# A pool-and-conv mixer inside a two-model kernel: pooled means moved from VectorE to GpSimd, with the last eight input tiles, the small pool products and the residual's norm in a new order

## Chip, cores and metric

The kernel runs on one core of a Trainium2 chip. The metric is the device time of one execution in microseconds. A profiled execution gives a span from its first to its last instruction; the execution's own time is a little longer, as the table below says.

## What is computed

The reference is a chain of two blocks over 256 positions of 1024 channels in f32: a first block (convolution, latent attention, a gated FFN and a final norm), then a second with a pool-and-conv mixer, an FFN, windowed attention and a mixture of eight experts. Only the mixer and what stands around it are touched:

```python
h = rmsnorm(x, ev_norm_mix); x = x + pool_conv_mixer(h, ...)
h = rmsnorm(x, ev_norm_ffn); x = x + swiglu(h, ...)

def pool_conv_mixer(h, w_in, pool_w, pool_scale, conv_w, w_out):
    proj = h @ w_in                                   # 1024 -> 2048
    u, gate_post, gate_pre, v = split(proj, 4)        # 512 channels each
    y_a = multiscale_pool(u, pool_w, pool_scale)
    y_b = gate_post * causal_depthwise_conv(gate_pre * v, conv_w)   # 3 taps
    return concatenate([y_a, y_b]) @ w_out            # 1024 -> 1024

def multiscale_pool(u, pool_w, pool_scale):           # windows 2, 4, 8, 16
    # per group of 128 channels with its window w:
    #   pooled = (sum of the last w positions) / min(t + 1, w) - u
    #   mixed  = pooled @ pool_w[group]               # 128 x 128
    return mixed * pool_scale
```

The `x` that enters the mixer is the first block's result under its final norm `norm_f_g`.

## The kernel before

**Layout.** Channels lie on the 128 partitions and the 256 positions along the free axis. A linear layer is a row of jobs; a job is one output tile of 128 channels x 256 positions in one PSUM bank (`jb(n)` is bank n mod 4). Each f32 product is made of three matmuls (`three`, L711 to L713): high by high, high by low and low by high, where high is an fp32r copy and low is what is left. A job of eight row tiles is 24 matmuls of 128x256.

**Weights.** They come in granules of 128x2048 f32 (1 MB) on SP's queue, six buffers deep. ScalarE writes the high half `whi` (L1144) and VectorE the low half `wlo` (L1516), three buffers deep. In the mixer a granule serves two jobs. `split_to(g)` makes all halves up to two granules beyond g. ScalarE's copy waits until the granule three back has been used up; SP's load into a buffer waits until VectorE's half of its last content is done. `split_past(n)` goes one further where job n is the last of its granule.

**Order of the mixer.** The order on every engine is written out by hand; engines meet at semaphores. Jobs `mix`+0 to 7 are pairs of gate_pre and v tiles; `mix`+8 to 15 are pairs of a gate_post and a u tile (called tiles 9 to 16 below). A job may start once the one four before it, which had its bank, has been drained (`drained`, `wait_drained`).
- *VectorE, first half.* After two statistics on bank 7 it makes `rsq` (L1795 to L1797). For each of four conv groups it drains two jobs (`pre`, L1605, and `z`, L1825) and makes the three taps in `zc` (L1827, L1829) and a scale (L1833). Between them stand `mid_norm` (a second variance, L1808, and the reciprocal `rlat`, L1813) and two calls of `normalise_two`, each of two L1803, which put the final norm of the first block into the residual `xres`.
- *VectorE, second half.* Four groups i = 0 to 3 (L1835 to L1862). Each makes its weight split, `yb` from PSUM (L1839), waits for ScalarE's high copy and writes the low half, drains u into `pu` (L1605), sums windows by doubling (L1854, i + 1 times, between `pa` and `pb`), multiplies by `recip` (L1856), subtracts (L1859, `pooled`), and waits for ScalarE's copy of the pool product before it writes its low half (L1861). `pu`, `pa`, `pb`, `pooled` and `yb` are one buffer each. Groups 2 and 3 also hold a `normalise_two`.
- *ScalarE.* For each group the weight copy, the high half of `yb` (L1322), and the scaled high half of the pool product from bank 6 (L1324).
- *TensorE.* Tile 9, tile 10, tile 11, pool product 0 (L914, `pool_mix`), tile 12, tile 13, pool product 1, and so on; product 3 stands after tile 16. Then the eight jobs of `mix_out`, whose operands are `mh` and `ml`.
- *Residual.* For each output tile VectorE adds PSUM to `xres` (L1743) and writes the low half of the next operand (L1558); ScalarE makes its high half and squares (L1162, L1163), and GpSimd sums the squares (L576). The next layer, `up2`, begins with two jobs together that need all eight operand tiles only at their end (`job_pair`).
- *GpSimd.* Sums of squares, here for the norms, DMAs of tables, and nothing between 410 and 487 us. It has no part in the mixer.

## Time and profile before

| | |
|---|---|
| median of 3 runs | 1789.27 us (1789.26 to 1790.92) |
| profiled execution, its own time | 1788.94 us |
| its span | 1787.1 us, mean granted TensorE clock 0.981 |
| TensorE matmul busy | 1704.0 us, 95%, 10076 instructions |
| VectorE busy | 1424.9 us, 80%, 1409 instructions |
| ScalarE busy | 1145.4 us, 64%, 1143 instructions |
| GpSimd busy | 148.4 us, 8%, 137 instructions |
| DMA | 513.47 MB, mean 287 GB/s |

PE is TensorE's matmuls, DVE VectorE, ACT ScalarE, POOL GpSimd, SP SyncE; L711 is line 711 of the kernel. Times are microseconds from the span's start. A matmul's shown duration (0.28 us at full clock) is longer than the spacing at which matmuls follow each other. The granted clock is a share of full speed; its two levels are 1.2 and 2.4 GHz. VectorE's instructions overlap by some 0.08 us where none waits for the other.

### The profile page before, as it was taken

Reading aid. Unit: us, or ns where it says so; the run is one execution under the profiler, and the core shown is the slowest. Engines: PE = TensorE matmul, PEld = TensorE weight load, DVE = VectorE, ACT = ScalarE, POOL = GpSimd, SP = SyncE. Lnnn points to the kernel's source line nnn. Section 1 sums busy time; section 2 is a strip of 40 time slices with the busy share of each in tenths; the row PEclk is TensorE's granted clock in tenths of the full one; section 3 lists DMA queues with packets and bytes.
Section 4 is the critical chain, followed back from the end, with each engine's and each line's share of the span. In section 5 each row is a group of like instructions: output and inputs, shape, how many; then the busy total and the mean of one; then the engine's idle time right before and its main releaser. Section 6 shows DMA issues by size and latency. Waiting matters only on the chain.

```text
span 1787.1 us, 26233 instructions
## 1 busy us (share of the span) xinstructions
PE 1704.0 (95%) x10076; PEld 1509.3 (84%) x10076; DVE 1424.9 (80%) x1409; ACT 1145.4 (64%) x1143; POOL 148.4 (8%) x137
## 2 busy tenths in 40 slices
PE   7899999998799998979999999999999999999994
PEld 6888999998799998877888888888888888888883
DVE  7896788857666656758888888888888888888886
ACT  5325577753344444647787787787877877878774
POOL 5000255410010001010000000000000000000000
PEclk9999999999899999999999999999999999999997
DMA  8334496594345557139999999999999999999994
GB/s 310 105 140 172 159 396 265 197 248 173 106 178 189 181 197 218 48 141 367 382 369 389 368 373 389 368 379 379 360 403 367 361 397 374 368 380 366 395 384 152
DMA packets 75037, 513.47 MB, mean 287 GB/s; under 512 B 7984, under 2 KB 8368, under 8 KB 16720
## 3 DMA queue, kind: packets, MB, share of 16 engines
q1 hardware_dynamic: 68688, 487.65, 71.4%
q0 software_dynamic: 6272, 24.76, 4.9%
q8 instruction: 52, 0.85, 0.2%
q14 instruction: 25, 0.20, 0.0%
HBM read 488.26 MB, written 24.12 MB: 287 GB/s over the span
## 4 chain that ended last, share of the span: by engine, by line
PE 87%; DVE 6%; ACT 3%; issue 1%; POOL 1%; DMA 1%; DVEq 0%; POOLq 0%; SPq 0%; ACTq 0%
PE psum L711 27%; PE psum L713 26%; PE psum L712 26%; PE psum L762 3%; DVE wlo L1516 2%; PE psum L1078 1%; ACT whi L1144 1%; DVE acc L1599 0%; PE psum L1049 0%; PE psum L953 0%; PE psum L840 0%; PE psum L861 0%; PE psum L801 0%; POOL ang L613 0%; DMA yrow<-expert_outs,idx 0%
## 5 line engine op out<-in xcount | busy, mean ns | idle before, releaser
L1516 DVE TENSOR_TENSOR wlo<-wraw,whi 128x2048 fp32r<-128x2048 f32 (+1 forms) x446 | 1014.5, 2278 | 210.6 <-ACT whi L1454 117.0
L1454 ACT ACTIVATE whi<-wraw 128x2048 fp32r<-128x2048 f32 x336 | 643.4, 1917 | 213.1 <-PE psum L713 213.1
L711 PE MATMUL psum<-whi,xgh 128*128 128x512 f32 x896 | 357.7, 399 | 1.8 <-DVE xgl L1516 1.8
L713 PE MATMUL psum<-whi,xgl 128*128 128x512 f32 x896 | 351.4, 392 | 0.0
L712 PE MATMUL psum<-wlo,xgh 128*128 128x512 f32 x896 | 349.1, 390 | 0.0
L711 PE MATMUL psum<-ah,whi 128*128 128x256 f32 x1064 | 307.3, 289 | 4.3 <-DVE u L1605 1.7
L712 PE MATMUL psum<-al,whi 128*128 128x256 f32 x1064 | 303.9, 286 | 0.0
L713 PE MATMUL psum<-ah,wlo 128*128 128x256 f32 x1064 | 303.6, 285 | 0.0
L1144 ACT ACTIVATE whi<-wraw 128x2048 fp32r<-128x2048 f32 x105 | 200.3, 1910 | 121.5 <-PE psum L713 121.5
L711 PEld LDWEIGHTS psum<-ah,whi 128*128 128x128 f32 x1064 | 207.3, 195 | 5.9 <-DVE wlo L1516 1.9
L712 PEld LDWEIGHTS psum<-al,whi 128*128 128x128 f32 x1064 | 207.1, 195 | 0.4
L713 PEld LDWEIGHTS psum<-ah,wlo 128*128 128x128 f32 x1064 | 207.0, 195 | 0.0
L713 PEld LDWEIGHTS psum<-whi,xgl 128*128 128x128 f32 x896 | 168.2, 188 | 39.3
L711 PEld LDWEIGHTS psum<-whi,xgh 128*128 128x128 f32 x896 | 168.5, 188 | 36.5 <-issue 2.0
L712 PEld LDWEIGHTS psum<-wlo,xgh 128*128 128x128 f32 x896 | 168.5, 188 | 35.0
L711 PE MATMUL psum<-whi,ath 128*128 128x512 f32 x448 | 177.8, 397 | 0.0
L713 PE MATMUL psum<-whi,atl 128*128 128x512 f32 x448 | 175.6, 392 | 0.0
L712 PE MATMUL psum<-wlo,ath 128*128 128x512 f32 x448 | 174.4, 389 | 0.0
L713 PEld LDWEIGHTS psum<-whi,atl 128*128 128x128 f32 x448 | 84.1, 188 | 19.6
L712 PEld LDWEIGHTS psum<-wlo,ath 128*128 128x128 f32 x448 | 84.2, 188 | 18.0
L711 PEld LDWEIGHTS psum<-whi,ath 128*128 128x128 f32 x448 | 84.2, 188 | 16.8
L711 PE MATMUL psum<-fh,whi 128*128 128x256 f32 x352 | 97.5, 277 | 0.0
(329 smaller groups left out, 2095.6 us busy)
## 6 DMA issues: line engine op xcount, KB each, us to landing
wraw<-weights SPq DMA_DIRECT2D x454, 1024.0 KB, 6.9
expert_rows<-zeros POOLq DMA_DIRECT2D x1, 8704.0 KB, 43.6
expert_outs<-ysb SPq DMA_DIRECT2D x9, 512.0 KB, 9.1
expert_outs<-zeros POOLq DMA_DIRECT2D x1, 4096.0 KB, 59.8
xgt<-expert_rows SPq DMA_DIRECT2D x8, 512.0 KB, 8.7
bias_rows<-ttab POOLq DMA_DIRECT2D x1, 3072.0 KB, 37.4
btab<-bias_rows POOLq DMA_DIRECT2D x2, 768.0 KB, 10.4
xres<-x SPq DMA_DIRECT2D x1, 1024.0 KB, 5.2
```

Of the source, the lines that this page charges most:

```text
L711: nc.tensor.matmul(out, lh, rh, start=start, stop=False)
L712: nc.tensor.matmul(out, lh, rl, start=False, stop=False)
L713: return nc.tensor.matmul(out, ll, rh, start=False, stop=stop)
L762: mm = nc.tensor.matmul(jb(n), wraw[:, g % NW, off:off + P], x[:, k, :], start=(k == 0), stop=(k == PLAN.jobs[n][-1][2]))
L1078: mm = nc.tensor.transpose(bank[6][:, i * P:(i + 1) * P], act_[:, i * P:(i + 1) * P], ident)
L1144: sc.activation(whi[:, i % NS, :], wraw[:, g % NW, :], ACT.Copy).then_inc(hi_done, 1)
L1454: sc.activation(whi[:, (GS + j) % NS, :], wraw[:, g % NW, :], ACT.Copy).then_inc(hi_done, 1)
L1516: return ve.tensor_tensor(dst, value, hi.bitcast(f32), SUB)
```

## The change

Group q of the second half is now channel group i = 3 - q, so the longest window comes first, and the u tile comes before the gate_post tile (`make_plan`). GpSimd zeroes the edges of `z`, `pu`, `pa` and `pb` and makes the window sums, the multiply and the subtract; each step waits for the one before. `pu` and `pooled` have a buffer for each group and `yb` two, at places that hold the first FFN's operands before. VectorE multiplies u by `rstd` into `pu`, and writes the low half of `yb` one group later and that of the pool product two groups later. TensorE makes products 0 and 1 between the tiles of groups 2 and 3, into banks 4 to 7 instead of bank 6, and products 2 and 3 between parts of the first two output tiles, whose rows are taken in the order 7, 6, 5, 3, 2, 4, 1, 0. ScalarE's copies follow that order. The reciprocal `rlat` stands after the four conv groups, and the four `normalise_two` stand in the residual of `mix_out`. VectorE no longer waits for `table_rep` and `late`; GpSimd waits for `late`.

```diff
@@ -151 +151 @@
         p.tile("ev_w_in_2", KD, spread(1536 + i * P, P))
-    for i in range(4):
+    for i in range(3, -1, -1):
+        p.tile("ev_w_in_2", KD, spread(i * P, P))
         p.tile("ev_w_in_2", KD, spread(512 + i * P, P))
-        p.tile("ev_w_in_2", KD, spread(i * P, P))
     linear("mix_out", "ev_w_out_2", KD, KD)
@@ -373 +373 @@
         PP = 16 + T
-        pa = place("pa", [P, PP], f32, 10 * KB + 256)
-        pb_ = place("pb", [P, PP], f32, 11 * KB + 512)
-        pu = place("pu", [P, PP], f32, 12 * KB + 768)
-        pooled = place("pooled", [P, T], f32, 14 * KB)
-        yb = place("yb", [P, T], f32, 15 * KB)
+        pu = place("pu", [P, 4, PP], f32, 40 * KB)
+        pa = place("pa", [P, PP], f32, 44 * KB + 512)
+        pb_ = place("pb", [P, PP], f32, 45 * KB + 768)
+        pooled = place("pooled", [P, 4, T], f32, 47 * KB)
+        yb = place("yb", [P, 2, T], f32, 51 * KB)
 
@@ -664 +666 @@
                     add(rlat[:], rlat[:], sq2[:, c % 2, :], summed2)
+            wait_job(pool, AT["down1"] + KD - 1)
+            pool.memset(z[:, :, 0:2], 0.0)
+            pool.memset(pu[:, :, 0:16], 0.0)
+            pool.memset(pa[:, 0:16], 0.0)
+            pool.memset(pb_[:, 0:16], 0.0).then_inc(edges_set, 1)
+            pool.wait_ge(late, 32)
+            pool.wait_ge(edges_set, 1)
+            windows = [0]
+
+            def window(ins):
+
+                ins.then_inc(window_step, 1)
+                windows[0] += 1
+                pool.wait_ge(window_step, windows[0])
+
+            for q in range(4):
+                i = 3 - q
+                pool.wait_ge(u_copied, q + 1)
+                src, dst = pu[:, i, :], pa
+                for step in range(i + 1):
+                    sh = 1 << step
+                    window(nc.gpsimd.tensor_tensor(dst[:, 16:PP], src[:, 16:PP], src[:, 16 - sh:PP - sh], ADD))
+                    src, dst = dst, (pb_ if dst is pa else pa)
+                window(nc.gpsimd.tensor_tensor(dst[:, 16:PP], src[:, 16:PP], recip[:, i, :], MUL))
+                nc.gpsimd.tensor_tensor(pooled[:, i, :], dst[:, 16:PP], pu[:, i, 16:PP], SUB).then_inc(pooled_done, 1)
+                pool.wait_ge(pooled_done, q + 1)
             for name in ("h4", "od"):
@@ -907 +935 @@
 
-            def pool_mix(i):
-                pe.wait_ge(pooled_done, i + 1)
-                if i:
-                    pe.wait_ge(m_lo, KD + 2 * i)
-                nc.tensor.matmul(bank[6][:, 0:T], poolw[:, i, :], pooled[:, :], start=True, stop=True).then_inc(pool_mm, 1)
-
-            for i in range(4):
-                job(AT["mix"] + 8 + 2 * i, ah, al)
-                if i:
-                    pool_mix(i - 1)
-                job(AT["mix"] + 9 + 2 * i, ah, al)
+            def pool_mix(q):
+
+                i = 3 - q
+                pe.wait_ge(pooled_done, q + 1)
+                if q == 3:
+                    pe.wait_ge(stat_read, stat[0])
+                nc.tensor.matmul(bank[4 + q][:, 0:T], poolw[:, i, :], pooled[:, i, :],
+                                 start=True, stop=True).then_inc(pool_mm, 1)
+
+            for q in range(4):
+                job(AT["mix"] + 8 + 2 * q, ah, al)
+                if q >= 2:
+                    pool_mix(q - 2)
+                job(AT["mix"] + 9 + 2 * q, ah, al)
+
+            mixed = (7, 6, 5, 3, 2, 4, 1, 0)
+
+            def mixed_ready(k):
+
+                return (p_lo, 4 - k) if k < 4 else (y_lo, 8 - k)
+
+            def mix_part(n, ks):
+
+                if ks[0] == mixed[0]:
+                    wait_drained(pe, n - 4)
+                for k in ks:
+                    g, off, _ = PLAN.jobs[n][k]
+                    once(lo_done, TURN[g] + 1)
+                    once(*mixed_ready(k))
+                    s = TURN[g] % NS
+                    mm = three(jb(n), whi[:, s, off:off + P], wlo[:, s, off:off + P], mh[:, k, :], ml[:, k, :],
+                               k == mixed[0], k == mixed[-1])
+                if ks[-1] == mixed[-1]:
+                    mm.then_inc(jobs_done, 1)
+                    at_piece[0] += 1
+
+            mix_part(AT["mix_out"], mixed[:3])
+            pool_mix(2)
+            mix_part(AT["mix_out"] + 1, mixed[:3])
+            mix_part(AT["mix_out"], mixed[3:6])
             pool_mix(3)
-
-            for i in range(KD):
-                job(AT["mix_out"] + i, mh, ml, lambda k: (m_lo, KD + (2 * k + 2 if k < 4 else 2 * (k - 4) + 1)))
+            mix_part(AT["mix_out"] + 1, mixed[3:6])
+            mix_part(AT["mix_out"], mixed[6:])
+            mix_part(AT["mix_out"] + 1, mixed[6:])
+            for i in range(2, KD):
+                job(AT["mix_out"] + i, mh, ml)
             job_pair(AT["up2"], ah, al, lambda k: (h_lo, 3 * KD + k + 1))
@@ -1315 +1374 @@
                 split_to(last_granule(AT["mix"] + 2 * i))
-            for i in range(4):
-                n = AT["mix"] + 8 + 2 * i
-                split_to(last_granule(n))
-                act.wait_ge(yb_done, i + 1)
-                sc.activation(mh[:, 4 + i, :], yb[:], ACT.Copy).then_inc(m_hi, 1)
-                act.wait_ge(pool_mm, i + 1)
-                sc.activation(mh[:, i, :], bank[6][:, 0:T], ACT.Copy, scale=pcol("ev_pool_scale_2", i)).then_inc(m_hi, 1)
+            def pool_hi(q):
+
+                i = 3 - q
+                act.wait_ge(pool_mm, q + 1)
+                sc.activation(mh[:, i, :], bank[4 + q][:, 0:T], ACT.Copy,
+                              scale=pcol("ev_pool_scale_2", i)).then_inc(p_hi, 1)
+
+            for q in range(4):
+                split_to(last_granule(AT["mix"] + 8 + 2 * q))
+                if q >= 2:
+                    pool_hi(q - 2)
+                act.wait_ge(yb_done, q + 1)
+                sc.activation(mh[:, 7 - q, :], yb[:, q % 2, :], ACT.Copy).then_inc(y_hi, 1)
+            pool_hi(2)
+            pool_hi(3)
             take("mix_out", lambda c: pcol("ev_norm_ffn_2", c))
@@ -1733 +1800 @@
 
-            def residual(phase, gain=None, bias=None):
+            def residual(phase, gain=None, bias=None, ahead=None):
 
...
                     split_to(last_granule(n))
+                    if ahead is not None:
+                        v.wait_ge(norm_done, i + 1)
                     wait_job(v, n)
@@ -1746 +1815 @@
                         operand_low(i - 1, gain)
+                    if ahead is not None and i % 2 == 0 and i + 2 < KD:
+                        ahead(i // 2 + 1)
                     if i < KD - 1:
@@ -1785 +1856 @@
 
-            v.wait_ge(table_rep, 16)
-            ve.memset(z[:], 0.0)
-            ve.memset(pb_[:], 0.0)
-            link(ve.memset(pu[:, 0:16], 0.0))
             split_to(last_granule(AT["mix"]))
@@ -1808 +1875 @@
                 v.sem_inc(stat_read, 1)
-                link(ve.memset(pa[:], 0.0))
-                v.wait_ge(rstd_sqrt, 2)
-                link(ve.reciprocal(rlat[:], var[:]))
 
...
                     mid_norm()
-                elif i > 1:
-                    normalise_two(i - 2)
                 n = AT["mix"] + 2 * i
@@ -1824 +1886 @@
                 wait_drained(v, n + 1)
+                if i == 0:
+                    v.wait_ge(edges_set, 1)
                 link(ve.tensor_scalar(zc[:, i, :], z[:, i, 0:T], pcol("ev_conv_w_2", i), None, MUL))
@@ -1831 +1895 @@
                 link(ve.tensor_tensor(zc[:, i, :], zc[:, i, :], rstd[:], MUL))
-            v.wait_ge(late, 32)
-            for i in range(4):
-                n = AT["mix"] + 8 + 2 * i
+            v.wait_ge(rstd_sqrt, 2)
+            link(ve.reciprocal(rlat[:], var[:]))
+
+            def gated_low(q):
+
+                v.wait_ge(y_hi, q + 1)
+                lo(ml[:, 7 - q, :], yb[:, q % 2, :], mh[:, 7 - q, :]).then_inc(y_lo, 1)
+
+            def pool_low(q):
+
+                i = 3 - q
+                v.wait_ge(p_hi, q + 1)
+                ve.scalar_tensor_tensor(ml[:, i, :], bank[4 + q][:, 0:T],
+                                        pcol("ev_pool_scale_2", i), mh[:, i, :].bitcast(f32), MUL, SUB).then_inc(p_lo, 1)
+
+            for q in range(4):
+                n = AT["mix"] + 8 + 2 * q
+                i = 3 - q
+                wait_job(v, n)
+                ve.tensor_tensor(pu[:, i, 16:PP], jb(n), rstd[:], MUL).then_inc(u_copied, 1)
+                v.wait_ge(u_copied, q + 1)
+                v.sem_inc(drained[n % 4], 1)
+                if q:
+                    gated_low(q - 1)
                 split_to(last_granule(n))
-                wait_job(v, n)
-                link(ve.tensor_tensor(yb[:], jb(n), zc[:, i, :], MUL))
-                v.sem_inc(drained[n % 4], 1)
-                v.sem_inc(yb_done, 1)
-                v.wait_ge(m_hi, KD + 2 * i + 1)
-                lo(ml[:, 4 + i, :], yb[:], mh[:, 4 + i, :]).then_inc(m_lo, 1)
-
-                if i:
-                    v.wait_ge(pooled_done, i)
-                if i >= 2:
-                    normalise_two(i)
-                drain(n + 1, pu[:, 16:PP])
-                wait_drained(v, n + 1)
-                src, dst = pu, pa
-                for step in range(i + 1):
-                    sh = 1 << step
-                    link(ve.tensor_tensor(dst[:, 16:PP], src[:, 16:PP], src[:, 16 - sh:PP - sh], ADD))
-                    src, dst = dst, (pb_ if dst is pa else pa)
-                link(ve.tensor_tensor(src[:, 16:PP], src[:, 16:PP], recip[:, i, :], MUL))
-                if i:
-                    v.wait_ge(pool_mm, i)
-                ve.tensor_tensor(pooled[:], src[:, 16:PP], pu[:, 16:PP], SUB).then_inc(pooled_done, 1)
-                v.wait_ge(m_hi, KD + 2 * i + 2)
-                ve.scalar_tensor_tensor(ml[:, i, :], bank[6][:, 0:T], pcol("ev_pool_scale_2", i),
-                                        mh[:, i, :].bitcast(f32), MUL, SUB).then_inc(m_lo, 1)
-            v.wait_ge(norm_done, KD)
-            residual("mix_out", lambda c: pcol("ev_norm_ffn_2", c))
+                if q >= 2:
+                    pool_low(q - 2)
+                wait_job(v, n + 1)
+                ve.tensor_tensor(yb[:, q % 2, :], jb(n + 1), zc[:, i, :], MUL).then_inc(yb_done, 1)
+                v.wait_ge(yb_done, q + 1)
+                v.sem_inc(drained[(n + 1) % 4], 1)
+            gated_low(3)
+            pool_low(2)
+            pool_low(3)
+            normalise_two(0)
+            residual("mix_out", lambda c: pcol("ev_norm_ffn_2", c), ahead=normalise_two)
             inverse_std(D, rstd)
...
```

## Rows read from the trace of the kernel before

**Rows 1.** The page, chain that ended last: share of the span by engine.

```profile
PE 87%; DVE 6%; ACT 3%; issue 1%; POOL 1%; DMA 1%; DVEq 0%; POOLq 0%; SPq 0%; ACTq 0%
```

**Rows 2.** Busy time by stretch: PE, PEld, DVE, ACT, POOL, clock, DMA share, GB/s.

```profile
407.00:440.00 33.00, 32.78 (x269) 32.36 (x267) 28.98 (x45) 12.58 (x11) 1.43 (x2) 1.00 0.43 150
440.00:484.00 44.00, 29.48 (x177) 28.07 (x177) 26.82 (x44) 11.58 (x14) 0.00 (x0) 0.77 0.31 106
...
540.00:640.00 100.00, 100.00 (x841) 100.00 (x840) 62.98 (x85) 43.69 (x53) 0.00 (x0) 1.00 0.52 180
```

**Rows 3.** Who waited for whom, 405 to 505 us: total, times, longest.

```profile
ACT mh L1324 <- PE psum L914: 17.8, 4, 5.7
ACT mh L1322 <- DVEq L1841: 17.5, 4, 8.9
...
PE psum L914 <- DVE pooled L1859: 14.5, 4, 5.1
```

**Rows 4.** TensorE in order of time: start, us, line, operation, idle before.

```profile
413.03 0.59 PE L904 MATMUL psum<-rlat,ones 128*128 128x256 f32 x2
...
439.94 0.28 PE L713 MATMUL psum<-ah,wlo 128*128 128x256 f32 x1
444.94 1.22 PE L914 MATMUL psum<-pooled,poolw 128*128 128x256 f32 x2 [4.71 <-DVE pooled L1859]
...
449.37 0.41 PE L712 MATMUL psum<-al,whi 128*128 128x256 f32 x1
...
475.83 1.22 PE L914 MATMUL psum<-pooled,poolw 128*128 128x256 f32 x2 [5.13 <-DVE pooled L1859]
...
483.65 0.28 PE L713 MATMUL psum<-mh,wlo 128*128 128x256 f32 x1
```

**Rows 5.** VectorE in order of time, 410 to 446 us.

```profile
413.02 0.92 DVE L1789 MEMSET z<- 128x1032 f32 x1 [0.16 <-issue]
...
414.29 0.42 DVE L1795 TENSOR_SCALAR var<-psum 128x256 f32<-128x256 f32 x1
...
422.66 2.29 DVE L1516 TENSOR_TENSOR wlo<-wraw,whi 128x2048 fp32r<-128x2048 f32 x1
...
439.48 2.29 DVE L1516 TENSOR_TENSOR wlo<-wraw,whi 128x2048 fp32r<-128x2048 f32 x1
```

**Rows 6.** Groups of instructions, 410 to 484 us: busy us, mean ns.

```profile
L1803 DVE SCALAR_TENSOR_TENSOR xres<-xres,par,rlat 128x256 f32<-128x256 f32 x8 | 3.5, 480 | 0.1
...
L1854 DVE TENSOR_TENSOR pa<-pu 128x256 f32<-128x256 f32 x4 | 1.7, 427 | 0.1
```

**Rows 7.** GpSimd, and VectorE where they meet, in order of time.

```profile
20.79 0.74 POOL L614 TENSOR_TENSOR ang<-ang 128x256 f32<-128x256 f32 x1
21.61 0.85 POOL L613 TENSOR_SCALAR ang<-ang 128x256 f32<-128x256 f32 x1
22.55 0.74 POOL L614 TENSOR_TENSOR ang<-ang 128x256 f32<-128x256 f32 x1
22.75 2.68 DVE L1516 TENSOR_TENSOR wlo<-wraw,whi 128x2048 fp32r<-128x2048 f32 x1
...
27.59 2.77 POOL L617 TENSOR_SCALAR ang<-ang 128x256 f32<-128x256 f32 x1
...
409.51 0.73 POOL L576 TENSOR_TENSOR rlat<-rlat,sq 128x256 f32<-128x256 f32 x1
...
486.33 2.29 DVE L1516 TENSOR_TENSOR wlo<-wraw,whi 128x2048 fp32r<-128x2048 f32 x1 [1.19 <-ACT whi L1144]
487.08 2.14 POOL L576 TENSOR_TENSOR ssum<-sq 128x256 f32<-128x256 f32 x1 [76.84 <-ACT sq L1163]
```

**Rows 8.** TensorE behind two earlier idle stretches, in order of time.

```profile
45.04 0.39 PE L711 MATMUL psum<-ah,whi 128*128 128x256 f32 x1 [1.68 <-DVE u L1605]
...
193.95 0.58 PE L711 MATMUL psum<-mh,whi 128*128 128x256 f32 x1 [2.58 <-DVE gates L1725]
```

**Rows 9.** ScalarE's weight copy in the loop, in order of time.

```profile
431.45 1.92 ACT L1144 ACTIVATE whi<-wraw 128x2048 fp32r<-128x2048 f32 x1 [4.32 <-PE psum L713]
```

More of the change, by code:

```diff
@@ L476, in program @@
         pooled_done, pool_mm, yb_done = sem("pooled_done"), sem("pool_mm"), sem("yb_done")
+        y_hi, y_lo, p_hi, p_lo = sem("y_hi"), sem("y_lo"), sem("p_hi"), sem("p_lo")
+        edges_set, window_step = sem("edges_set"), sem("window_step")
         table_mm, table_out, table_rep, bias_ready = sem("table_mm"), sem("table_out"), sem("table_rep"), sem("bias_ready")
```

## The prediction, made before the change was run

> **What bounds the kernel now.** The page first: TensorE holds 87% of the chain that ended last [rows 1]; only stretches where it is idle or slow can give time. The table by stretches then shows where one is [rows 2]: from 540 to 640 us it is busy all of 100 us with 841 matmuls (0.12 us each, 2.88 us for a tile of 24) at granted clock 1.00; from 440 to 484 us, where the change works, it is busy 29.5 of 44 us at a mean clock of 0.77, with VectorE at 26.8 and the DMA engines at 0.31, so neither is full: a stretch of waits. The waits name them [rows 3]: TensorE's pool products (L914) wait 14.5 us, four times, for `pooled` of VectorE; ScalarE's copies wait 17.8 us for those products and 17.5 us for `yb`. The order of time shows the loop [rows 4]: the last matmul before the first product starts at 439.94, the first and the fourth product at 444.94 and 475.83 after 4.71 and 5.13 us of idleness, and output tiles 1 and 2 end at 483.9. At 449.37 a matmul still takes 0.41 us, against 0.28 before the idle stretch: the lower level, 1.2 GHz. VectorE starts a weight split at 439.48 [rows 5], and in this loop needs 9 to 11 us a group (two tiles) where TensorE needs 5.8.
>
> So from the end of mixer tile 11 (440.0) to the end of output tile 2 (483.9) pass 43.9 us. At full clock and without waits it would be 5 mixer tiles and 2 output tiles, 7 x 2.88 = 20.2 us, and four products of 0.66, 2.6 us: 22.8. **21.1 us are to be had**, 14.5 of idleness and 6.6 of lower clock.
>
> **Part by part.**
>
> *Before the eight tiles.* Three memsets go from VectorE to GpSimd: 0.92 us [rows 5] and two small ones. What is late next is TensorE's statistic, which ends at 413.6 [rows 4] against VectorE's start on it at 414.29 [rows 5]: gain 0.6. The reciprocal of 1.75 us moves behind the fourth conv group; the split that followed it at 422.66 then waits for ScalarE, which makes its high half only after its second square root, so all of this gives 0.65. Two pairs of L1803 (0.48 us each) go too, 1.8 us [rows 6], but the reciprocal comes back ahead of the first u tile: VectorE takes that tile at about 439.0. TensorE, which waited there three times for a drain, ends tile 11 at 439.3: **0.7 us gained**. GpSimd's four memsets (bound below by nothing; above by the 0.92 us of the whole `z`, 3.7 in all) begin behind its sum that ends at 410.2 [rows 7] and are wanted at 416.9: they cost nothing under 6.7 us together; beyond that VectorE's first conv step would wait for them.
>
> *Pooled means.* Ten window adds, four multiplies and four subtracts leave VectorE, 18 x 0.43 = 7.7 us [rows 6]. On GpSimd an add of this size takes 0.74 us alone, and with the wait behind it the next starts after 0.82 (20.79 and 21.61) [rows 7]. The multiply and the subtract of two tensors get the price of the add: nearest row, same operands; bounds 0.74 and the 2.77 of a step that met a split. Groups run with windows 16, 8, 4, 2: 6, 5, 4 and 3 steps, 14.8 us unhindered. They meet VectorE's splits: the sum at 487.08 took 2.14 us, ending 0.6 after the split begun at 486.33, and a split begun at 22.75, 0.2 us after a GpSimd add, took 2.68 instead of 2.29 [rows 7]. One waits until the other has finished, in either direction; operations with a PSUM input (0.41) keep their time.
>
> The Trainium skill (SBUF — State Buffer, SBUF: two separate sides) calls this port pair an exclusive lock on which the loser fully blocks; the rows agree.
>
> *First chain.* u tile 0 is copied at 439.4; VectorE starts the split of the mixer's seventh granule (m6) at the same moment. First add ends at 441.7 + 0.6 = 442.3; adds 2 to 4 end at 443.1, 444.0, 444.8; the multiply falls under the next split (VectorE 444.4 to 446.9, held up 0.25) and ends at 447.5; the subtract at 448.3. TensorE meanwhile does tiles 12 and 13 of the mixer and is out of work at 445.0, since pool product 0 stands ahead of tile 14. **Idle for 3.3 us.** Afterwards the clock: earlier, an idle stretch of 2.58 us was followed by a first matmul of 0.58 us, one of 1.68 us by one of 0.39 [rows 8]. 3.3 lies beyond the longer, so I take the lower level for about 4.6 us, as behind 444.94 [rows 4]: some 19 matmuls at 0.213 instead of 0.12 and a product at 1.2: **2.2 us**. If the clock stays up, that is 0; both ends go into the range.
>
> *Following chains.* TensorE goes on at 448.3: product 0 (1.2), tile 14 until 454.2, tile 15 until 457.0, product 1, tile 16 until 460.5, three of eight rows of output tile 1 (9 matmuls, 1.1) until 461.6, product 2, three rows each of output tiles 2 and 1 until 464.4, product 3, and the rest until 467.6. GpSimd's second chain runs from 448.3 with one split in between, five steps, to 454.3: hidden. The third has its u since 447.7, four steps, 457.4: hidden by 4 us. The fourth gets its u from tile 15 at 457.6, meets a split until 460.8 and is done at 462.2: hidden by 2.
>
> *VectorE and ScalarE in the loop.* VectorE has per group a split (2.29) and four short operations (0.42 to 0.48, as in [rows 6]): 4.0 us, under 5.8 even with 0.6 for each of two meetings. What it now queues behind p_hi and y_hi, ScalarE delivers a group later; ScalarE has 1.92 [rows 9] and two short copies a group. Its waits for the pool product sit behind the split, and product 0 (448.9) is over before that split is (449.5). The SP queue: each load is released by a split's end, so loads come earlier with the rest; share 0.31 becomes about 0.5, which is what the later stretch has at full pace [rows 2]. No DMA is added or moved, and GpSimd's next ones belong to the attention, far behind. VectorE's wait for the bias table goes; that write had landed.
>
> *Residual's norm.* Four pairs of L1803, formerly two among the conv groups and two in the loop, now stand in the residual: one pair (0.88) before tile 1, the others behind tiles 0, 2, 4. The residual then has per two tiles a split 2.29, two adds and two lows at 0.42 to 0.48 (1.8), a pair 0.96, with one more meeting with GpSimd's sums (0.6): 5.65 against 5.76 of TensorE. Tight: VectorE enters it at 466, behind the last pooled low, and the last lows come about 0.3 us after up2's first pair of jobs wants them (before, they were there in time). **0.3 us lost.**
>
> **Sum.** 43.9 us become 22.8 + 3.3 + 2.2 = 28.3, gain 15.6; plus 0.7, less 0.3: **16.0 us**. Against the profiled execution's 1788.94 us that is 1773.0; the median of the runs, 1789.27, lies 0.3 above it, so I give **1773.2**. All behind runs on TensorE at full pace [rows 2] and moves forward as a block.
>
> **Rivals.**
> *Gapless.* GpSimd slips its first add in ahead of m6, no later step meets a split, or the idleness stays short enough for the clock. Chain: 6 x 0.82 = 4.9 us, done at 444.3 to 445.5. Gain 21.1 + 0.7 - 0.3, less at most 2 for single meetings: -19.5 to -21.5, 1768 to 1770. Against it: a split stands right behind the u copy in the queue, and ScalarE's half for it is ready.
> *The port eats it.* Each step on GpSimd excludes VectorE's two-SBUF-input work, so the 14.8 us come back on VectorE in place of the 7.7 removed: 7.1 us more, gain 9, **1780**. For: both directions show in [rows 7]. Against: VectorE has some 1.8 us a group to spare, and its PSUM operations pass. The Trainium skill (Perfetto Trace Analysis, Optimizing Scalar/DVE Operations) says that moving work between these two might not help because of the shared port; by that the time would be this one or worse.
> *Slower.* The chain of GpSimd, in order and linked, becomes the bound: all steps near the price of a collision, 2.5 us (between 2.14 and 2.77). 439.4 + 18 x 2.58 = 485.8, then product, ScalarE, VectorE and the rows of the output tiles left, some 5.2: 491 against 483.9, **+7, 1796**. It decides from about 2 us a step. Against: VectorE's splits fill 2.3 of 5.8 us, and most steps must run between them.
> *Does nothing.* Something else, such as ScalarE's order, holds the loop at its old pace: 1789. Nothing in [rows 3] speaks for it once `pooled` is gone.
>
> **Chances.** Forecast 0.58 (1770.5 to 1776.5), gapless 0.13, port 0.20, slower 0.05, nothing 0.04. The range takes forecast, gapless and most of port: 1768 to 1780.5. A measurement tells about 0.2% (3.6 us) from no change: faster 0.92, same 0.04, slower 0.04.
>
> **What the profile after should show.** Right: L914 idle before it about 3.3 us in one place, none over 1 elsewhere; 440 to 484 at clock about 0.95; GpSimd's 18 steps at 0.74, five or six of them 2 us or more; output tile 2's end near 467.6; up2 in step 16 us earlier. Wrong: product 1 to 3 waiting for POOL (port or slower), splits well over 2.7 us, or TensorE waiting for `al` at up2 by more than 1 us.

## The result and the profile after

The changed kernel takes **1773.3 us** (median of 4 runs, 1771.28 to 1774.46) against 1789.26 us (4 runs, 1789.16 to 1790.92), a ratio of 0.9906 with a 95% interval of [0.9894, 0.9918]: 16.0 us less, where 1773.2 was forecast. Its profiled execution took 1774.46 us (span 1772.3, clock 0.981), 14.5 less than that of before. TensorE holds 89% of the chain that ended last, against 87% in [rows 1].

The table by stretches, columns as in [rows 2]:

```profile
407.00:440.00 33.00, 33.00 (x275) 32.89 (x274) 25.87 (x38) 12.59 (x11) 1.66 (x6) 1.00 0.45 160
440.00:484.00 44.00, 41.08 (x333) 40.66 (x332) 32.19 (x43) 20.64 (x27) 27.34 (x23) 0.96 0.46 168
540.00:640.00 100.00, 100.00 (x850) 100.00 (x849) 60.97 (x77) 44.10 (x51) 1.48 (x2) 1.00 0.53 184
```

From 440 to 484 us TensorE is busy 41.1 of 44 us, not 29.5, with 333 matmuls in place of 177, and its mean clock is 0.96, not 0.77. The waits from 405 to 490 us show what is left:

```profile
ACT mh L1389 <- DVE yb L1926: 19.5, 4, 9.3
DVE wlo L1583 <- ACT whi L1203: 13.2, 10, 2.7
...
PE psum L944 <- POOL pooled L693: 2.9, 1, 2.9
...
ACT mh L1381 <- PE psum L944: 2.7, 2, 2.1
...
PE psum L739 <- DVE al L1625: 1.0, 1, 1.0
```

Against [rows 3]: TensorE waits for `pooled` once and 2.9 us, not four times and 14.5; ScalarE waits 2.7 us for the small products, not 17.8. ScalarE's long wait for `yb` is still there (19.5) and costs nothing by these rows: VectorE makes the low half from this `mh` one group later and waits 0.5 us for it once, and TensorE never waits for it. The one new wait of TensorE is for `al`, 1.0 us. GpSimd in order of time has all 18 steps of the pooled means; the first group, the other long steps and the last:

```profile
440.26 2.74 POOL L690 TENSOR_TENSOR pa<-pu 128x256 f32<-128x256 f32 x1 [29.12 <-DVE pu L1917]
443.07 0.61 POOL L690 TENSOR_TENSOR pb<-pa 128x256 f32<-128x256 f32 x1
443.76 0.71 POOL L690 TENSOR_TENSOR pa<-pb 128x256 f32<-128x256 f32 x1
444.55 0.73 POOL L690 TENSOR_TENSOR pb<-pa 128x256 f32<-128x256 f32 x1
445.37 2.65 POOL L692 TENSOR_TENSOR pa<-pb,recip 128x256 f32<-128x256 f32 x1
448.10 0.73 POOL L693 TENSOR_TENSOR pooled<-pa,pu 128x256 f32<-128x256 f32 x1
...
450.35 2.54 POOL L690 TENSOR_TENSOR pa<-pb 128x256 f32<-128x256 f32 x1
...
458.40 2.67 POOL L692 TENSOR_TENSOR pb<-pa,recip 128x256 f32<-128x256 f32 x1
461.14 0.74 POOL L693 TENSOR_TENSOR pooled<-pb,pu 128x256 f32<-128x256 f32 x1
```

Four steps take 2.54 to 2.74 us, each begun 0.03 to 0.6 us behind the start of a weight split of VectorE; the other fourteen take 0.61 to 0.74. TensorE behind the first product:

```profile
448.88 0.70 PE L944 MATMUL psum<-pooled,poolw 128*128 128x256 f32 x2 [2.92 <-POOL pooled L693]
...
449.53 0.29 PE L740 MATMUL psum<-al,whi 128*128 128x256 f32 x1
449.65 0.38 PE L741 MATMUL psum<-ah,wlo 128*128 128x256 f32 x1
449.83 0.42 PE L739 MATMUL psum<-ah,whi 128*128 128x256 f32 x1
...
456.65 0.59 PE L944 MATMUL psum<-pooled,poolw 128*128 128x256 f32 x2
...
463.55 0.60 PE L944 MATMUL psum<-pooled,poolw 128*128 128x256 f32 x2
```

Beside [rows 4]: there the first, third and fourth product took 1.22 us, at the lower level, and the second 0.70. Here the one behind the idle stretch takes 0.70, the others 0.59 to 0.60, and the lower level (0.42 us a matmul) begins only at 449.7 and ends at 453.0.

**The stage measured by itself.** To read the experiments I use one length in each profile: from the start of the mixer's second statistics product on TensorE (L904 before, L932 after) to that of up2 (L801, L829). It holds all that the change touches but the memsets of the edges on GpSimd (410.9 to 411.2 us). What stands behind it is read in two lengths that no edit touches: from there to VectorE's first work on the attention's keys (`kk`), 190.3 to 190.4 us in every profile, and from `kk` to its first work on the experts' result rows (`yrow`), called "attention to experts" below.

| | before | after |
| --- | --- | --- |
| start | 413.03 | 413.70 |
| to the end of tile 11 | 27.03 | 26.34 |
| from there to the end of output tile 2 | 44.07 | 26.35 |
| from there to up2's statistic | 22.71 | 23.72 |
| **stage** | **93.81** | **76.41** |
| attention to experts | 1075.1 | 1076.7 |

The stage gained 17.4 us. It began 0.7 later, attention to experts took 1.6 more, the rest of the span 0.2 and what lies around the span 0.4: 14.5 are left in the profiled execution. In the thirteen profiles of this document the stage begins anywhere between 411.9 and 416.2 us, so a difference of 0.7 there says nothing of the change.

### The profile page after: what moved, and what is told of

It reads as the page before. It is cut to its first block, busy times and chain, and to the rows that moved or that the text cites. A ratio compares the mean times of both kernels' runs of the same rounds, so it can differ in the third digit from the quotient of the medians.

```text
span 1772.3 us, 26239 instructions
## 1 busy us (share of the span) xinstructions
PE 1701.3 (96%) x10076; PEld 1507.5 (85%) x10076; DVE 1416.5 (80%) x1387; ACT 1145.0 (65%) x1143; POOL 168.7 (10%) x159
## 4 chain that ended last, share of the span: by engine, by line
PE 89%; DVE 5%; ACT 2%; POOL 2%; issue 1%; DMA 1%; DVEq 0%; POOLq 0%; SPq 0%; ACTq 0%
PE psum L739 27%; PE psum L741 27%; PE psum L740 26%; PE psum L790 3%; PE psum L1137 1%; DVE wlo L1583 1%; ACT whi L1203 1%; DVE acc L1666 0%; PE psum L1108 0%; PE psum L1012 0%; PE psum L868 0%; PE psum L889 0%; PE psum L829 0%; POOL ang L615 0%; PE psum L1019 0%
## 5 line engine op out<-in xcount | busy, mean ns | idle before, releaser
L739 PEld LDWEIGHTS psum<-whi,ath 128*128 128x128 f32 x448 | 84.3, 188 | 16.3
```

Source lines behind the costliest of these rows:

```text
L739: nc.tensor.matmul(out, lh, rh, start=start, stop=False)
```

## The experiments

Of each kernel the median of 4 runs is given (of 10 for the eighth), its ratio to the kernel before on the same chip with the 95% interval, and the stage of its profile. The kernel before, beside them, had medians of 1788.92, 1790.02 and 1790.48 us.

**1. The means back on VectorE, all else kept**

```diff
# GpSimd: the loop over q with its window steps and waits is gone; on VectorE, behind each u copy
+                if q == 0:
+                    v.wait_ge(late, 32)
+                src, dst = pu[:, i, :], pa
+                for step in range(i + 1):
+                    link(ve.tensor_tensor(dst[:, 16:PP], src[:, 16:PP], src[:, 16 - sh:PP - sh], ADD))
...
+                link(ve.tensor_tensor(dst[:, 16:PP], src[:, 16:PP], recip[:, i, :], MUL))
+                ve.tensor_tensor(pooled[:, i, :], dst[:, 16:PP], pu[:, i, 16:PP], SUB).then_inc(pooled_done, 1)
```

> The changed kernel with its order, buffers and late products, but the 18 window steps back on VectorE, each group's behind its u copy. Theory A (the order pays: products two groups late, own buffers): product 0 is ready some 6 us earlier (6 steps of 0.46 us, no port), TensorE instead waits about 1.7 us for the low half of the seventh granule, which now stands behind 2.8 us of steps; VectorE has 6.8, 6.3, 5.8 and 5.4 us a group against 5.76. About the changed kernel's time, 1773 (1771 to 1776). Theory B (the gain is the work taken off VectorE): VectorE becomes the bound again, most of the gain goes, 1780 to 1789.

1773.86 us (1771.92 to 1775.47), ratio 0.9914 [0.9897, 0.993]; stage 76.70, 0.3 more than after. The waits and the stretch:

```profile
PE psum L718 <- DVE wlo L1562: 2.2, 1, 2.2
...
PE psum L718 <- DVE al L1604: 1.0, 1, 1.0
...
PE psum L718 <- DVE ml L1562: 0.6, 1, 0.6
```

```profile
440.00:484.00 44.00, 40.27 (x322) 39.34 (x320) 38.37 (x60) 20.87 (x29) 8.45 (x5) 0.96 0.48 168
```

No wait for `pooled` at all: VectorE has the first group ready in time, and in exchange is late with one split (2.2 us) and with one `ml` (0.6). It is busy 38.4 us of 44 rather than 32.2, and that still suffices. **The engine is not what pays.** What pays lies in the order, the buffers and the lateness of the small work. The lateness is priced by number 2 and the norm pairs by 7 and 8; the order of the windows and the buffers of their own were not tried alone.

**2. Products and low halves one group late**

```diff
-                if q >= 2:
-                    pool_mix(q - 2)
+                if q >= 1:
+                    pool_mix(q - 1)
...
+            pool_mix(3)
```

with the same for `pool_hi` on ScalarE and `pool_low` on VectorE.

> Means on GpSimd as in the changed kernel, but each product one group earlier, where the kernel before has them (product 3 behind tile 16), and ScalarE's and VectorE's halves of it likewise. Theory A: product 0 stands behind tile 11 and waits for the GpSimd chain until 448.8: some 9 us idle, and two later products wait about a microsecond or two: 7 us slower than the changed kernel, 1780 (1777 to 1784). Theory B (work off VectorE pays, the place of the products does not): 1773 to 1775.

1778.9 us (1778.48 to 1782.27), ratio 0.9947 [0.993, 0.9963]; stage 82.89, **6.5 us longer** than after.

```profile
PE psum L944 <- POOL pooled L693: 10.5, 2, 8.7
```

GpSimd's chain is as long as before, but TensorE meets it one tile pair earlier and waits 8.7 us at once. A first chain of 8.6 us (440.26 to 448.8 in the changed kernel) can be hidden only behind more than one group of 5.8 us. With the means on VectorE, where number 1 has the first group ready 2.7 us after its first window step, one group might be enough; that was not tried, so the 6.5 us hold for the chain on GpSimd.

**3. The first product behind tile 14**

```diff
-                if q >= 2:
-                    pool_mix(q - 2)
+                if q == 3:
+                    pool_mix(1)
                 job(AT["mix"] + 9 + 2 * q, ah, al)
+                if q == 2:
+                    pool_mix(0)
```

> Changed kernel with product 0 behind tile 14 instead of ahead of it. Theory C (TensorE's idle stretch of 2.9 us and the lower clock behind it, 1.4 us, are simply lost time): 4 us faster, 1769. Theory D (the GpSimd chain of all four groups, without a gap from the first u copy to the last subtract, some 22 us, sets when the stretch ends): the idle time moves to product 1 (about 2.5 us, for its pooled at 454.4) and the time stays, 1773.

1773.19 us (1771.55 to 1773.99), ratio 0.9908 [0.9892, 0.9925]; stage 75.88, 0.5 less. Product by product on TensorE:

```profile
448.41 0.70 PE L944 MATMUL psum<-pooled,poolw 128*128 128x256 f32 x2
...
454.08 1.22 PE L944 MATMUL psum<-pooled,poolw 128*128 128x256 f32 x2 [2.11 <-POOL pooled L693]
```

The first product no longer waits, the second does (2.1 us). The position of the product is not the limit; the second chain runs straight behind the first, and both are late by when the first began.

**4. Subtract only.** This kernel leaves the window additions and the multiply by `recip` out of the pooled means; one GpSimd step a group is left.

```diff
-                for step in range(i + 1):
+                for step in range(0):
...
-                nc.gpsimd.tensor_tensor(pooled[:, i, :], dst[:, 16:PP], pu[:, i, 16:PP], SUB).then_inc(pooled_done, 1)
+                nc.gpsimd.tensor_tensor(pooled[:, i, :], recip[:, i, :], pu[:, i, 16:PP], SUB).then_inc(pooled_done, 1)
```

> Leaves out the window adds and the multiply: GpSimd only subtracts u from the reciprocal counts, 4 steps instead of 18, so the pooled means are other values. This prices the whole chain and its meetings at the port. Theory D: product 0 no longer waits, clock stays up, splits are not held up: 4 us faster than the changed kernel, 1769 to 1770. Rival (the port eats it): splits and low halves were held up much more than the trace shows, 7 us or more faster, 1766 or less. If nothing of it counted: 1773.

1769.54 us (1769.16 to 1772.44), ratio 0.9894 [0.9877, 0.991]; stage 72.66. So the fourteen steps left out, with their meetings and the clock, cost **3.75 us** of the stage and no more. The stretch is at full clock throughout, and `al` is waited for 0.3 us:

```profile
440.00:484.00 44.00, 42.97 (x351) 42.14 (x351) 34.37 (x47) 23.21 (x32) 16.04 (x11) 1.00 0.51 183
```

**5. The reciprocal back where VectorE idles.** The change moved it (1.75 us) from the middle of the conv groups to ahead of the first u copy. VectorE after, in order of time:

```profile
419.92 0.42 DVE L1875 TENSOR_SCALAR var<-psum 128x256 f32<-128x256 f32 x1
422.63 2.29 DVE L1583 TENSOR_TENSOR wlo<-wraw,whi 128x2048 fp32r<-128x2048 f32 x1 [2.29 <-ACT whi L1203]
...
437.87 1.75 DVE L1899 RECIPROCAL rlat<-var 128x256 f32<-128x256 f32 x1
439.66 0.42 DVE L1917 TENSOR_TENSOR pu<-psum,rstd 128x256 f32<-128x256 f32 x1
```

It idles for 2.29 us at 420.3, and holds up the u copy by 1.75 at 437.87.

```diff
                 v.sem_inc(stat_read, 1)
+                v.wait_ge(rstd_sqrt, 2)
+                link(ve.reciprocal(rlat[:], var[:]))
...
-            v.wait_ge(rstd_sqrt, 2)
-            link(ve.reciprocal(rlat[:], var[:]))
```

> Changed kernel with the reciprocal of 1.75 us back in the middle norm, where VectorE has 2.3 us idle for ScalarE's weight copy. Theory D (what sets the stretch's end is when the GpSimd chain begins): the first u copy comes 1.75 us earlier, the first subtract likewise, product 0 waits 1.2 us instead of 2.9, the clock stays up or falls for less: from the two statistics products on, the stretch is 2.7 us shorter than 76.4 (73.7), 1770.5. Rival (that position of the reciprocal is free because the chain is not what counts): 1773.

1770.26 us (1767.06 to 1772.95), ratio 0.9888 [0.9871, 0.9904]; stage 73.55. VectorE in this kernel:

```profile
422.17 1.75 DVE L1879 RECIPROCAL rlat<-var 128x256 f32<-128x256 f32 x1 [0.48 <-ACT var L1374]
424.04 2.29 DVE L1583 TENSOR_TENSOR wlo<-wraw,whi 128x2048 fp32r<-128x2048 f32 x1
...
439.28 0.42 DVE L1917 TENSOR_TENSOR pu<-psum,rstd 128x256 f32<-128x256 f32 x1
```

Counted from each stage's start, the u copy comes at 24.2 us instead of 26.0. TensorE waits for `pooled` 1.2 us instead of 2.9, and the clock stays at 1.00 from 440 to 484. Up to the fourth small product TensorE waits 1.7 us less and gets 1.5 us back from the clock, and loses 0.35 around the third product, for which it now comes a little early: 2.85, the whole difference of the stages.

**6. As 5, and the first group's six steps on VectorE**

```diff
+                if q == 0:
+                    v.wait_ge(late, 32)
...
+                    link(ve.tensor_tensor(dst[:, 16:PP], src[:, 16:PP], recip[:, i, :], MUL))
+                    ve.tensor_tensor(pooled[:, i, :], dst[:, 16:PP], pu[:, i, 16:PP], SUB).then_inc(first_pooled, 1)
```

(behind the group's `yb`; GpSimd's loop starts at q = 1.)

> As e4_reciprocal_back, and the window of 16 (six steps, the first group) on VectorE behind that group's yb; the other three stay on GpSimd, with a semaphore of its own for the first product. Theory D: product 0 is there before TensorE is, GpSimd's chain begins 2.8 us earlier with the second group and ends earlier; no idle stretch over 1 us in the loop, stretch 72.7 us, 1769.5. Rival (VectorE is full again as soon as one window is back): 1773 or more.

1772.62 us (1771.84 to 1774.27), ratio 0.9905 [0.9889, 0.9922]; stage 73.43, against 73.55 of number 5. The 1.2 us of waiting for `pooled` went, and two waits of 0.5 and 0.7 us for VectorE's `ml` took its place. The further 0.85 us expected did not come.

**7. The norm pairs in the loop again**

```diff
+                normalise_two(q)
...
-            normalise_two(0)
-            residual("mix_out", lambda c: pcol("ev_norm_ffn_2", c), ahead=normalise_two)
+            v.wait_ge(norm_done, KD)
+            residual("mix_out", lambda c: pcol("ev_norm_ffn_2", c))
```

> Changed kernel with the four pairs of the residual's norm taken out of the residual and one put behind each group's yb in the loop. Theory D: the loop's pairs meet GpSimd's steps at the port and put its chain back by about a microsecond, the residual is lighter but VectorE enters it as late: 1 us slower, 1774. Rival (the place of the norm among the output tiles costs TensorE its 1.1 us wait at the next layer, and the loop has room): 1 us faster, 1772.

1773.8 us (1773.46 to 1774.48), ratio 0.9914 [0.9898, 0.9931]; stage 78.14, 1.7 longer than after. TensorE waits for `pooled` 3.5 us and still 1.1 us for `al`. The median does not show the 1.7: outside of the stage this kernel had 2.5 us less than after in its profile (1074.2 for attention to experts).

**8. The kernel before, with the norm pairs among the output tiles alone**

```diff
-                elif i > 1:
-                    normalise_two(i - 2)
...
-                if i >= 2:
-                    normalise_two(i)
...
-            v.wait_ge(norm_done, KD)
-            residual("mix_out", lambda c: pcol("ev_norm_ffn_2", c))
+            normalise_two(0)
+            residual("mix_out", lambda c: pcol("ev_norm_ffn_2", c), ahead=normalise_two)
```

> The kernel before with one part of the change alone: the four pairs of the residual's norm among the output tiles. The chain of waits in the loop goes through VectorE, so two pairs out of it (1.6 us) and two ahead of it (1.8 us, part of it hidden) should come off, less 0.9 in the residual: 2 to 3 us faster than the kernel before, 1786 to 1787. If the residual cannot take them: as before or slower.

1786.43 us (1783.62 to 1789.82, 10 runs), ratio 0.9984 [0.9974, 0.9994]; stage 89.60, **4.2 less** than before, more than the 2 to 3 expected.

```profile
PE psum L914 <- DVE pooled L1859: 13.1, 4, 6.3
```

The order of the loop is otherwise untouched and the wait for `pooled` is nearly whole (13.1 for 14.5 us). Of the 4.2 us, 3.3 lie between the end of tile 11 and that of output tile 2, where the waits are 1.4 us shorter and the mean clock is higher (0.84 instead of 0.77 from 440 to 484 us). A further 0.6 us is a faster pace of the last six output tiles, which nothing here ties to the edit, and the rest lies ahead of tile 11's end. That VectorE's shorter queue gives the 3.3 is argued, not shown. TensorE does not wait for `al` in this kernel. So this part alone is up to a quarter of the stage's gain while VectorE bounds the loop, and 1.7 us (number 7) once it doesn't.

**9 to 11. Reciprocal back and first product later; 5 again; the changed kernel again,** on one chip. Number 9 has the diffs of 3 and 5 together.

> The reciprocal back in the idle stretch and the first small product behind tile 14. Theory F (what is left is bound by the end of GpSimd's uninterrupted chain): the second product stands behind tile 15, wanted at about 453.3 where the second group's subtract ended at 454.2 with the reciprocal back, so a wait of about 0.9 us takes the place of 1.36, no lower clock, stage (first mixer statistic to up2's) 73.1 against 73.55 of the reciprocal alone, 0.4 gained, not to be told in the medians. Theory G (the two changes add in full): 75.88 less 2.86, and so 73.0 as well but with the wait gone from both products. Told apart by whether L944 still waits for POOL, 0.7 to 1.1 us once (F), or under 0.3 (G).

> The reciprocal back in the idle stretch, once more, beside the changed kernel on the same chip. If its 2.9 us in the stage are real for the whole: median 2.5 to 3.2 us below the changed kernel's. If what lies behind the stage takes them back: under 1 us.

> The changed kernel itself beside the two others, for the comparison: 1771 to 1775 us, stage within 0.5 us of 76.41 if the stage repeats from one execution to the next and the spread of 1 to 3 us lies outside of it; elsewhere if the spread is in the stage.

| | median (lowest to highest) | ratio | stage |
| --- | --- | --- | --- |
| 9 both | 1770.09 (1769.39 to 1772.9) | 0.9886 [0.987, 0.9903] | 73.40 |
| 10 reciprocal back | 1771.25 (1769.69 to 1773.94) | 0.9899 [0.9883, 0.9916] | 73.57 |
| 11 changed kernel | 1773.01 (1771.17 to 1773.62) | 0.99 [0.9884, 0.9917] | 76.39 |

In number 9 the first product no longer waits; the second and the third do:

```profile
PE psum L944 <- POOL pooled L693: 1.2, 2, 0.7
```

That is 0.74 us at the second and 0.45 at the third, where one wait of about 0.9 was expected; the stage is 0.15 below number 5, so the two edits don't add: what is left is GpSimd's chain. Numbers 10 and 11 **repeat their stage within 0.02 us** (73.55 and 73.57, 76.41 and 76.39), while attention to experts differs between the two profiles of the changed kernel by 1.8 (1076.7, 1074.9). The 1.8 us between the medians of 10 and 11 is less than the 2.5 to 3.2 I expected; over both sets of runs (8 each, taken at different times) the medians are 1770.4 and 1773.1, 2.7 apart, close to the stage's 2.86. The intervals of the ratios overlap, so the stage carries that finding, not the medians.

Numbers 5 and 9 have the lowest medians of the kernels that compute the whole mixer, 1770.3 and 1770.1 us, and stages 2.9 and 3.0 us below the changed kernel's; the intervals of their ratios still overlap with its own.

## Why the prediction was right, step by step

**What bounded the kernel** was right: the wait for `pooled` in the loop. Number 2 brings 10.5 of the 14.5 us of that wait back, and 6.5 of the 17.4 us of stage; number 1 shows that in the new order the engine doesn't matter. The prediction had no way to say that of the engine: it priced the whole change, not its parts. Had the means stayed on VectorE, its own per-group sum (4.0 us, with 7.7 us more over four groups, so 5.9 on average against TensorE's 5.8) would have said "just enough", and that is what number 1 measured. What of the other 10.9 us of stage is due to the order of the windows, to the buffers or to VectorE's waits for ScalarE's copies of the products (6.8 us before, from 410 to 484) is open.

**Before the eight tiles:** 0.7 forecast, 0.69 measured (27.03 to 26.34). But the step took the reciprocal's new place as part of a gain and stopped at TensorE. It noted that the split at 422.66 would wait for ScalarE, so that 1.75 us of free time came up there, and that the reciprocal "comes back ahead of the first u tile", and did not follow this to the chain that starts with that tile. There it costs 2.9 us (numbers 5, 10). That is the costliest thing the prediction had before it and didn't name.

**First chain.** The first u copy was forecast to end at 439.4 and ended at 440.1; the chain was to end at 448.3 and ended at 448.8, the product following at 448.88. The stage itself began 0.67 later, so counted from its start the copy fits within 0.1 us and the chain's end within 0.2. Price of a step 0.74 (measured 0.61 to 0.74), of one that met a split up to 2.77 (measured 2.54 to 2.74), the two in the first chain as forecast. Idle 3.3 us, measured 3.1 from the end of tile 13 to the product. Four steps met a split, not five or six.

**Following chains:** second, third and fourth forecast done at 454.3, 457.4 and 462.2; measured 454.5, 457.6 and 461.9. All hidden, as said.

**Clock:** forecast 2.2 us. Tile 14 and its start took 4.55 us against 2.88 at full pace, of which 0.18 is the step behind the product: 1.5 us. The stretch of lower level was shorter (449.7 to 453.0, not 4.6 us) and left the product out. **Products:** priced at 0.66 each, the distance from one product's start to the next matmul's in [rows 4]'s stretch, which ran at the lower level. At full clock that distance is 0.24 to 0.35, and the matmul behind takes 0.18 longer to its successor: 0.53 for the first and 0.43 for the others, 1.8 in place of 2.6. With these the middle stretch is 20.2 + 3.1 + 1.5 + 1.8 = 26.6, measured 26.35, forecast 28.3. These two, the clock (0.7) and the products (0.8), are the mis-sized terms; I counted a duration of the slow stretch in a sum of the fast one. Most of the 0.25 left over is output rows that ran at 0.113 us a matmul where 0.12 was reckoned.

**Residual and up2:** 0.3 us lost forecast, 1.0 measured (22.71 to 23.72). The six output tiles took 16.3 us instead of 17.0, and from there to up2's statistic 7.4 instead of 5.75, with waits of 1.03 and 0.11 us for `al`. A wait for `al` of more than 1 us was among the prediction's signs of being wrong; it came, just. The cause I gave, the norm pairs, is wrong: number 7 has none there and waits 1.1 us, number 8 has them and waits not at all. In the changed kernel the last output tile ends on TensorE at 482.7, and VectorE, which still has a split to do, adds it at 485.55:

```profile
477.14 2.29 DVE L1583 TENSOR_TENSOR wlo<-wraw,whi 128x2048 fp32r<-128x2048 f32 x1 [0.47 <-ACT whi L1203]
479.35 0.42 DVE L1812 TENSOR_TENSOR xres<-psum,xres 128x256 f32<-128x256 f32 x1
...
482.47 2.29 DVE L1583 TENSOR_TENSOR wlo<-wraw,whi 128x2048 fp32r<-128x2048 f32 x1 [0.47 <-ACT whi L1203]
484.68 0.42 DVE L1812 TENSOR_TENSOR xres<-psum,xres 128x256 f32<-128x256 f32 x1
485.01 0.61 DVE L1625 SCALAR_TENSOR_TENSOR al<-xres,par,ah 128x256 fp32r<-128x256 f32 x1
485.55 0.41 DVE L1812 TENSOR_TENSOR xres<-psum,xres 128x256 f32<-128x256 f32 x1
```

It is 2.8 us behind. In number 7, with no pair near, it is 2.9 behind (tile ended 484.9, add at 487.78); before, the add at 501.29 stood 0.2 us behind its tile, VectorE having waited for it. ScalarE in the same stretch of the changed kernel shows what holds VectorE:

```profile
475.20 1.91 ACT L1203 ACTIVATE whi<-wraw 128x2048 fp32r<-128x2048 f32 x1
...
479.80 0.51 ACT L1221 ACTIVATE ah<-xres,par 128x256 fp32r<-128x256 f32 x1 [1.99 <-DVE xres L1812]
480.22 0.40 ACT L1222 ACTIVATE sq<-xres 128x256 f32<-128x256 f32 x1
480.53 1.91 ACT L1203 ACTIVATE whi<-wraw 128x2048 fp32r<-128x2048 f32 x1
```

ScalarE's weight copy stands behind the high half and the square of a tile, these wait for VectorE's add, the add stands behind the split, and the split waits for the copy before. That is a ring of 5.3 us for two tiles (475.20 to 480.53) in which neither engine waits for TensorE. It starts with the copy at 464.55, which follows ScalarE's half of the fourth small product. So the fourth product sets the end of the stage: in all ten profiles where up2 waits for `al`, that wait ends 22.1 to 22.2 us after the start of the fourth product, and up2's statistic begins 26.5 to 26.6 us after it (463.55, 485.68 and 490.11 here; 465.71, 487.91 and 492.34 in number 7). Between these kernels the stages differ by when the fourth product starts, to 0.1 us. Before, and in numbers 2 and 8, TensorE reaches the end of its output tiles later than the ring does, and doesn't wait. What the prediction had wrong here is the path: it followed VectorE's own work (5.65 us for two tiles) and not the ring with ScalarE. An edit that starts the ring earlier was not tried.

The six output tiles took 17.0 us before and in numbers 4, 6 and 9 (0.118 us a matmul) and 16.3 in all other profiles (0.113), at a granted clock of 1.00 in both. Where up2 waits for `al` the wait takes the difference up (0.3 instead of 1.03 us); before, it counts, so 0.6 of the 17.4 us come from it. Why they differ I leave open.

**Everything behind moves as a block:** wrong by 1 to 3 us in a single execution. The attention, where matmuls are few, got a lower clock in this profile:

```profile
688.30:708.30 20.00, 12.85 (x53) 10.49 (x52) 11.16 (x28) 8.61 (x25) 0.00 (x0) 0.59 0.43 131
...
773.60:788.60 15.00, 8.53 (x53) 8.23 (x53) 11.25 (x41) 6.50 (x12) 4.73 (x3) 0.66 0.35 113
```

The same part of the program before (a few matmuls more fall into the fixed lengths):

```profile
705.00:725.00 20.00, 11.49 (x61) 9.70 (x60) 11.15 (x28) 8.97 (x25) 0.00 (x0) 0.83 0.42 134
...
790.00:805.00 15.00, 7.13 (x49) 6.64 (x47) 12.27 (x43) 7.85 (x14) 5.73 (x4) 0.77 0.39 138
```

Over the thirteen profiles attention to experts takes 1074.2 to 1077.5 us. Two profiles of one and the same kernel differ by 1.8 (after and number 11), so much of it is a spread of single executions. The four kernels with the reciprocal back all lie high, though, at 1076.9 to 1077.5 (numbers 5, 6, 9, 10), and one profile of each cannot exclude that this edit has a part in it. What sets it is open. So that the forecast of 1773.2 came out to 0.1 us is luck: a stage 1.4 us better than forecast met a rest that was 2.9 us worse than the block, in this execution; the medians, 16.0 apart, sit between.

**Rivals.** *Gapless* fell: the first step met a split, as the queue had said; number 4, with one step a group left, shows what it would have given, 3.75 us of stage at most. *The port eats it* fell: 4 meetings of about 1.9 us each on GpSimd, and on VectorE one split lengthened by 0.4 (457.77, 2.70), another by 0.07 and one `ml` by 0.2 (448.49, 0.61). Summed over the stage, VectorE's instructions take 62.3 us against 69.1 in number 1, where the eighteen steps take 7.65: 0.8 us came back, not 14.8. Here the Trainium skill (Perfetto Trace Analysis, Optimizing Scalar/DVE Operations) was right in its caution that the move may not help: 0.3 us of stage. How much of that is the port is not shown: the two meetings lengthen the first chain by 3.9 us, more than the 2.9 us that TensorE waits for it, while number 1 loses 2.2 and 0.6 us at VectorE's own work. *Slower* needed some 2 us a step; the mean was 1.1 (14 of about 0.7, 4 of about 2.65). *Does nothing*: no. The chances of the rivals add up to 0.91 for faster and 0.05 for slower, where the prediction's last sum has 0.92 and 0.04; nothing hangs on it.

**The exclusion at the port** is shown in each of the four long steps: the split begun at 440.23 runs to 442.5 and the step begun at 440.26 ends at 443.0, 0.5 us behind it, as in [rows 7], and the other three end 0.5 to 0.6 us behind their splits; the Trainium skill's rule (SBUF — State Buffer, SBUF: two separate sides) holds here. VectorE's operations with a PSUM input kept their 0.42 us beside GpSimd (443.00 and 447.92, both inside GpSimd's chain).

## What to carry to other kernels

Before moving a side chain to another engine, count how many groups late its consumer may be: here one more group of slack was worth 6.5 us to a chain of 8.6 us, the other engine 0.3. Then follow the moved work to the *start* of that chain: a 1.75 us operation put ahead of the chain's first input cost 2.9 us, while the same operation in a place where its engine waits anyway was free. Follow it to its *end* as well: the last small product started a ring of two other engines, and the stage ended a fixed 26.5 us behind it. And compare variants by a stage between two fixed instructions: it repeated to 0.02 us in both kernels that were profiled twice, where whole runs of them differ by 3 to 6.

## What the runs showed of the hardware that was not expected

- Behind a gap of 2.92 us TensorE's first product ran at full speed (0.70 us) and the lower level came 0.8 us later, for 3.3 us. In number 3 a gap of 2.11 us was followed by a product of 1.22 us, at the lower level (1.2 GHz) at once. In number 7 a gap of 3.53 us was followed by 1.22 us at once too. In number 5 a gap of 1.2 us left the clock at 1.00 from 440 to 484. So the length of the gap alone does not tell what follows.
- GpSimd additions of 256 elements a partition took 0.61 us in some places where 0.74 was the rule (443.07 against 444.55), with a start-to-start distance of 0.69 to 0.82.
- GpSimd's four memsets took 0.11 to 0.15 us each, where 0.92 was the upper bound for one; they were done by 411.2.
